# Gated mixer trunk, one core: the stage between the last block and the output projection rearranged, low parts of mixed tiles 4 to 7 on POOL

## The reference, cut to what matters

```
mixed = sum over n of sigmoid(h @ w_gate[n] + b_gate[n]) * (o[n] @ w_branch[n])
x = x + gate1 * (mixed @ w_out)
x = x + gate2 * conv_ffn(rms_norm(x) * (1 + scale2) + shift2)
out = rms_norm(x)
```

## Time and profile before

| | us |
|---|---|
| median of 3 runs (lowest, highest) | 2003.59 (2002.2, 2004.47) |
| the profiled execution, its own time | 2004.98 |
| span of its profile | 2003.1 |
| PE busy in the span | 1891.8 (94%) |
| POOL busy | 909.0 (45%) |
| DVE busy | 930.9 (46%) |
| ACT busy | 471.6 (24%) |

### The profile page before, as it was taken

How to read it: one execution, slowest core, us unless ns; L and a number is a source line. 1 busy time by engine, 2 the same in 40 slices (tenths; PEclk the granted TensorE clock), 3 DMA queues, 4 the chain that set the end, 5 groups by cost and what they waited for, 6 DMA issues and landing times.

```text
span 2003.1 us, 33657 instructions
## 1 busy us (share of the span) xinstructions
PE 1891.8 (94%) x14012; PEld 1511.2 (75%) x14012; DVE 930.9 (46%) x1470; ACT 471.6 (24%) x732; POOL 909.0 (45%) x1100
## 2 busy tenths in 40 slices
PE   4998899998999999999997799999999999999995
PEld 2886677767788878887885677788888888888884
DVE  5455669855454544544543824532332322323325
ACT  4313444442221312212212302410110100101003
POOL 1675456521332323323232475365564655646554
PEclk7999899999999999999998899999999999999998
DMA  8472211221312212212115631011111111111112
GB/s 324 136 236 84 74 53 64 96 98 53 98 39 88 78 54 93 67 60 85 44 60 194 229 107 53 21 43 52 45 50 52 42 52 52 42 52 43 52 42 84
DMA packets 70497, 164.98 MB, mean 82 GB/s; under 512 B 6000, under 2 KB 31088, under 8 KB 70384
## 3 DMA queue, kind: packets, MB, share of 16 engines
q1 hardware_dynamic: 62896, 144.45, 22.0%
q10 hardware_dynamic: 7488, 18.88, 2.6%
HBM read 133.95 MB, written 29.36 MB: 82 GB/s over the span
## 4 chain that ended last, share of the span: by engine, by line
PE 46%; POOL 22%; issue 19%; DVE 5%; ACT 3%; DMA 3%; SPq 1%; POOLq 0%; ACTq 0%; DVEq 0%
PE gbank L550 32%; POOL w_hi L467 11%; POOL w_lo L471 11%; PE mbank L867 3%; DMA fa<-in_w_ada 1%; DVE fa L1730 1%; PE gbank L867 1%; PE mbank L624 1%; DMA fa<-mix_scr 1%; PE gbank L645 1%; DVE fa L1669 1%; PE mbank L790 1%; PE mbank L964 1%; POOL fa L530 1%; PE mbank L633 1%
## 5 line engine op out<-in xcount | busy, mean ns | idle before, releaser
L467 POOL TENSOR_TENSOR w_hi<-w_raw,zero 128x256 fp32r<-128x256 f32 (+1 forms) x528 | 402.7, 793 | 1014.0 <-PE gbank L550 820.5
L550 PE MATMUL gbank<-h_hi,w_hi 128*128 128x512 f32 x1696 | 675.7, 398 | 10.0 <-POOL w_lo L471 6.1
L550 PE MATMUL gbank<-h_hi,w_lo 128*128 128x512 f32 x1696 | 675.2, 398 | 0.0
L550 PE MATMUL gbank<-h_lo,w_hi 128*128 128x512 f32 x1696 | 671.9, 396 | 0.0
L471 POOL TENSOR_TENSOR w_lo<-w_raw,w_hi 128x256 fp32r<-128x256 f32 (+1 forms) x528 | 467.2, 915 | 10.3
L550 PEld LDWEIGHTS gbank<-h_hi,w_hi 128*128 128x128 f32 x1696 | 320.8, 189 | 91.9 <-issue 19.0
L550 PEld LDWEIGHTS gbank<-h_hi,w_lo 128*128 128x128 f32 x1696 | 320.7, 189 | 70.2 <-issue 3.1
L550 PEld LDWEIGHTS gbank<-h_lo,w_hi 128*128 128x128 f32 x1696 | 320.9, 189 | 66.8 <-issue 1.4
L1088 PE MATMUL mbank<-ra,w_hi 128*128 128x512 f32 x640 | 197.1, 389 | 0.0
L1088 PEld LDWEIGHTS mbank<-ra,w_hi 128*128 128x128 f32 x640 | 120.1, 188 | 24.9
L2115 DVE SCALAR_TENSOR_TENSOR fa<-mbank,mod,fa 128x1024 f32<-128x1024 f32 x40 | 51.4, 1284 | 169.2 <-PE mbank L1088 169.2
(11 more groups left out here) (324 smaller groups left out, 2078.9 us busy)
## 6 DMA issues: line engine op xcount, KB each, us to landing
w_raw<-in_w_tail SPq DMA_DIRECT2D x74, 512.0 KB, 3.6
fa<-in_w_ada SPq DMA_DIRECT2D x48, 512.0 KB, 5.2
w_raw<-in_w_in SPq DMA_DIRECT2D x26, 512.0 KB, 3.6
p_scr<-fa ACTq DMA_DIRECT2D x20, 512.0 KB, 2.6
w_raw<-in_w_mix SPq DMA_DIRECT2D x16, 640.0 KB, 3.8
fa<-in_xT SPq DMA_DIRECT2D x16, 512.0 KB, 8.5
fa<-p_scr SPq DMA_DIRECT2D x8, 1024.0 KB, 5.7
w_raw<-in_w_gate SPq DMA_DIRECT2D x16, 512.0 KB, 4.9
```

What stands on the lines that cost most here:

```text
L467: last = pool.tensor_tensor(hi[:, c], raw[:, c], zero[:, 0:1].to_broadcast([P, w]), ALU.add)
L550: mm = pe.matmul(gb[bank], w, r, start=(q == 0), stop=(q == 3 * ks - 1))
```

## The change

It rewrites the stage after the last block, and leaves the arithmetic as it is.

- **Places in `fa`.** The tiles are laid out anew, so that what is dead before the last block ends lies in tiles 0 to 11. The `mix` tile is tile 7: the last block's mixed columns stay there, as tile m = 7.
- **o.** The first 896 columns (blocks 0 to 6) are loaded during block 7 (`o_in`), and their high and low parts are made by ACT and DVE inside block 7; the last 128 columns come straight from the block's tiles. The stores of block 7 are gone.
- **Loads.** The first four gate tiles (now tiles 8 to 11) and the mixed tiles are loaded during block 7 as well, in SP's queue between the `w_branch` units.
- **Branch weights.** Units 60 and 61 are split into `h_hi`/`h_lo` tiles 6 and 7, which are free until mixed tiles 6 and 7 are made, so they wait for no product. Unit 62 then waits for product 4, unit 63 for product 8.
- **First output tile.** Its matmuls go to `mbank`, and those for mixed tile k = 0, 1, 2 stand between products: after products 11, 13 and 15; k = 3 to 7 follow. In the PE's queue `first_out_tile(0)`, which waits for the split of unit 62, stands ahead of product 12.
- **SP's queue.** Unit 61 is fetched after the gate tiles for products 4 to 7, unit 62 after those for 8 to 11 (the last waits for the sum of product 7), unit 63 after those for 12 to 15 (the last waits for the sum of product 11).
- **Low parts of the mixed tiles.** DVE makes those of tiles 0 to 3; POOL makes those of tiles 4 to 7, each in four pieces of 256 columns, in its queue behind the split of unit 63.

```diff
+        O_COLS = (NB - 1) * P
+        o_room = [r_.rearrange("p (t c) -> p t c", t=2) for r_ in (flat[:, 0:2 * O_COLS], flat[:, 2 * S:2 * S + 2 * O_COLS])]
+        GATE_TILE = 8
...
@@ SP
-            for n in range(2):
-                unit("w_branch", n, n, U_BR + n)
-            block_out(NB - 1)
-            sp.wait_ge(sem("gated"), 4 * NB)
-            sp.wait_ge(sem("block_stored"), 48 * NB)
-            sp.wait_ge(sem("sig_stored"), 64 * NB)
...
+            sp.wait_ge(sem("block_stored"), 48 * (NB - 1))
+            sp.wait_ge(sem("pblk_read"), NB)
+            o_in(0)
+            sp.wait_ge(sem("rw_p3"), at("rw_p3", NB - 1))
+            o_in(1)
+            unit("w_branch", 0, 0, U_BR)
...
+            sp.wait_ge(sem("r3"), at("r3", NB - 1))
+            sp.wait_ge(sem("sig_stored"), 64 * (NB - 1))
             for s_ in range(4):
+                if s_ == 2:
+                    sp.wait_ge(sem("gated"), 4 * NB)
+                gate_in(s_ // 2, s_)
+            sp.dma_start(fa[:, 4:7, :], mix_scr[4:7].rearrange("t p c -> p t c")).then_inc(sem("mix_in1"), 16)
+            sp.wait_ge(sem("o_lo"), 2)
+            sp.dma_start(fa[:, 0:4, :], mix_scr[0:4].rearrange("t p c -> p t c")).then_inc(sem("mix_in0"), 16)
+            unit("w_branch", 1, 1, U_BR + 1)
+            unit("w_branch", 2, 0, U_BR + 2)
             for un in range(1, 4):
-                if un >= 2:
-                    unit("w_branch", un, un % 2, U_BR + un)
                 for s_ in range(4):
                     sp.wait_ge(sem("mixed"), 4 * un + s_ - 3)
+                    if un == 3 and s_ == 2:
+                        sp.wait_ge(sem("sig_stored"), 64 * NB)
+                    gate_in(2 * un + s_ // 2, s_)
+                if un == 1:
+                    unit("w_branch", 3, 1, U_BR + 3)
+                else:
+                    unit("w_tail", un - 2, un % 2, U_OUT + un - 2)
@@ POOL
             for un in range(4):
-                used = (sem("gb2_full"), U_BR - 1 + un) if un < 2 else (sem("br_full"), 4 * un - 4)
-                split(U_BR + un, un % 2, 16 * ((U_BR + un) // 2 + 1), used=used)
+                to = None if un < 2 else (h_hi[:, 4 + un, :], h_lo[:, 4 + un, :])
+                split(U_BR + un, un % 2, 16 * ((U_BR + un) // 2 + 1), used=(sem("gb2_full"), min(U_BR - 1 + un, U_BR)), to=to)
+            def mixed_lo(k):
+                pool.wait_ge(sem("mixed_lo"), k)
+                pool.wait_ge(sem("mixed_hi"), k + 1)
+                for c in [slice(n * 256, (n + 1) * 256) for n in range(4)]:
+                    last = pool.tensor_tensor(h_lo[:, k, c], fa[:, k, c], h_hi[:, k, c].bitcast(F32), ALU.subtract)
+                last.then_inc(sem("mixed_lo"), 1)
             for m in OUT_ORDER:
...
-                    used = (sem("br_full"), 12 + 4 * m) if m < 2 else (sem("half_done"), 2 * m - 2)
+                    used = (sem("br_full"), 4 + 4 * m) if m < 2 else (sem("half_done"), 2 * m - 2)
...
                 split(u, u % 2, 16 * (u // 2 + 1), used=used, to=to)
+                if m == 1:
+                    for k in range(KT // 2, KT):
+                        mixed_lo(k)
@@ PE
+            def branch_product(t):
...
+                if t % 4 == 0:
+                    pe.wait_ge(sem("w_split"), U_BR + 1 + un)
+                if t < 2:
+                    pe.wait_ge(sem("o_lo"), 3 + br)
+                else:
+                    pe.wait_ge(sem("gated"), 4 * NB + t - 1)
...
+            def first_out_tile(k):
+                if k == 0:
+                    pe.wait_ge(sem("w_split"), OUT_POS[0] + 1)
...
+                pe.wait_ge(sem("mixed_lo"), k + 1)
...
+            for t in range(2 * KT):
+                branch_product(t)
+                if t >= 11 and t % 2:
+                    first_out_tile(t // 2 - 5)
+            for k in range(3, KT):
+                first_out_tile(k)
@@ ACT, block 7 only: ahead of gate_raw(4), behind gate_raw(6), ahead of gate_raw(7)
+                    act.wait_ge(sem("gb1_full"), 4 * NB)
+                    for n in range(2):
+                        act.wait_ge(sem(f"o_in{n}"), 16)
+                        act.activation(ra[:, 4 * n:4 * n + 2, 0:O_COLS], o_room[n], ACT.Copy).then_inc(sem("o_hi"), 1)
...
+                    last_o_hi(0, "gd_o", gd["o"])
...
+                    last_o_hi(1, "rw_o", rw["o"])
@@ DVE, block 7 only: o_lo(0) behind new_values(0), o_lo(1) behind next_state(0), last columns behind gd_o and rw_o
+                def o_lo(n, nth, cols, o_):
+                    dve.wait_ge(sem("o_hi"), nth)
+                    dve.tensor_tensor(ra[:, 4 * n + 2:4 * n + 4, cols], o_, ra[:, 4 * n:4 * n + 2, cols].bitcast(F32),
+                                      ALU.subtract).then_inc(sem("o_lo"), 1)
...
-                if m:
+                if 1 <= m <= KT // 2:
                     mixed_lo(m - 1)
-            mixed_lo(KT - 1)
```

More of the change, by code:

```diff
@@ L234, in room, with rooms @@
             return names[name]
[L236 to L247, removed]
+        rw, gd = {}, {}
+        def rooms(table, prefix, *entries):
+            for n_, c_ in entries:
+                table[n_] = room(prefix + n_, c_)
@@ L1011, in out_unit @@
-            def out_unit(m, slot, first):
+            def branch_product(t):
+                m, br = divmod(t, 2)
+                un, c = m // 2, m % 2 * 512 + br * 256
+                hi, lo = (w_hi[:, un, :], w_lo[:, un, :]) if un < 2 else (h_hi[:, 4 + un, :], h_lo[:, 4 + un, :])
+                if t % 4 == 0:
[4 more added lines that the diff above has]
+                    pe.wait_ge(sem("gated"), 4 * NB + t - 1)
+                for hf in range(2):
+                    for k in range(2):
+                        for which in range(3):
+                            w = (lo if which == 2 else hi)[:, c + k * P:c + (k + 1) * P]
+                            r = ra[:, 4 * br + (2 if which == 1 else 0) + k, hf * HALF:(hf + 1) * HALF]
+                            mm = pe.matmul(gb[2 * br + hf], w, r, start=(k == 0 and which == 0), stop=(k == 1 and which == 2))
+                mm.then_inc(sem("br_full"), 1)
@@ new lines, in first_out_tile @@
+            def first_out_tile(k):
+                if k == 0:
+                    pe.wait_ge(sem("w_split"), OUT_POS[0] + 1)
+                    pe.wait_ge(sem("rw_rno"), at("rw_rno", NB - 1))
+                    pe.wait_ge(sem("rw_o"), at("rw_o", NB - 1))
+                pe.wait_ge(sem("mixed_lo"), k + 1)
+                for hf in range(2):
+                    for which in range(3):
+                        w = (w_lo if which == 2 else w_hi)[:, 0, k * P:(k + 1) * P]
+                        r = (h_lo if which == 1 else h_hi)[:, k, hf * HALF:(hf + 1) * HALF]
+                        mm = pe.matmul(mb[hf], w, r, start=(k == 0 and which == 0), stop=(k == KT - 1 and which == 2))
+                    if k == KT - 1:
+                        mm.then_inc(sem("half_done"), 1)
@@ L1451, in _ @@
                 gate_raw(6)
+                if not ahead:
+                    last_o_hi(0, "gd_o", gd["o"])
                 act.wait_ge(sem("rw_m2"), at("rw_m2", i))
@@ L1977, in _ @@
                     prep_bonus(i + 1)
+                else:
+                    o_lo(0, 1, slice(0, O_COLS), o_room[0])
                 dve.wait_ge(sem("rw_dec"), at("rw_dec", i))
@@ L1981, in _ @@
                     prep_decayed(i + 1)
+                else:
+                    o_lo(1, 2, slice(0, O_COLS), o_room[1])
                 new_values(1)
@@ L1995, in _ @@
                 dve.tensor_tensor(gd["o"], gd["o"], gd["z"], ALU.mult).then_inc(done("gd_o", i), 1)
+                if not ahead:
+                    o_lo(0, 3, slice(O_COLS, S), t2(gd["o"]))
                 dve.wait_ge(sem("rw_rno"), at("rw_rno", i))
```

105 lines of the change are left out of this document (41 added, 64 removed).

## The result

| | before | after |
|---|---|---|
| median (lowest, highest), us | 2004.03 (2002.2, 2006.35) | 1982.91 (1980.62, 1983.97) |
| ratio, 95% interval | | 0.9892 [0.9875, 0.991] |
| profiled execution: span, us | 2003.1 | 1982.2 |

The forecast was 1980.9 with a range of 1976 to 1988. The kernel is 21 us faster, and the stage accounts for all of it: from the start of `gate_raw(7)` to DVE's reading of the second half of output tile 0 it was 90.27 us and is 69.27. In what follows this is "the stage". Where the two readings are one row of x2, the second starts 0.66 us after the row.

A forecast was written before the change was run, and what follows sets the result against it. The PE bounds the kernel, but in the stage after the last block it loses time to three waits (26.3 us) and a lower clock. 2004.98 - 22.7 = 1982.3, with the median 1.4 below: 1980.9 us, range 1976 to 1988.

The forecast's parts named there:

- Part 1: Block 7: loading and converting o there costs nothing, with 0.5 and 0.4 us of cover; product 0 starts at 1079.2.
- Part 2: The products: PE paces two tiles, then DVE at 6.04 to 6.47 us each; the 7.2 us wait is gone.
- Part 3: Unit 62, before product 12: its split takes 9.0 us, PE waits 6.3 us and loses the clock for 12 matmuls.
- Part 4: Unit 63 and POOL's four low parts end at 1144.5, the stage at 1146.0: a gain of 22.7 us.
- The price of a shared operation: POOL's work beside DVE: each DVE operation with both operands in SBUF costs POOL 0.96 us.
- Part 5: Output projection after the stage: unit 64 is ready 0.3 us before the PE needs it, so nothing is given back.
- 1 (hindered all the way): POOL's split and low parts cost what contended rows say: gain 10.6 us, time 1993.0; chance 0.14.
- 2 (not hindered): POOL's splits and low parts are not slowed by DVE: gain 27.5 us, time 1976.1; chance 0.09.
- 3: Block 7 or the output projection pays, through late low parts of o or unit 64: some 4 us, 1985; chance 0.13.
- 4: Short PE waits before most products hold the clock at 1.2 GHz from product 4 on: 36 us, 2017; chance 0.04.

The follow-up runs named there:

- e7_o_behind: Changed kernel, but ACT and DVE make the high and low parts of o's first 896 columns behind block 7, units 59 and 60 fetched first: 1993.33 us.
- e10_changed: The changed kernel without any edit, timed again on the same chip as `e11_both_again`: 1983.35 us, ratio to before 0.9898.
- e1_low_dve: Changed kernel, but DVE makes all eight low parts of the mixed tiles and POOL none: 1981.05 us, ratio to before 0.9877.
- e6_no_interleave: Changed kernel, but the matmuls of output tile 0 stand behind all 16 products: 1980.13 us in one run.
- e2_psum_sum: Changed kernel, but DVE's sum reads an idle PSUM bank in place of the mixed tile, so the result is wrong: 1976.87 us in one run.
- e9_shared: Changed kernel, units 62 and 63 fetched four gate tiles earlier, POOL making low parts of tiles 4 and 5, DVE those of 6 and 7: 1976.42 us.
- e5_slots: Changed kernel, but branch weights are split into the two old slots and the first output tile stands behind all products: 1983.34 us in one run.
- e4_both: Changed kernel, but units 62 and 63 fetched four gate tiles earlier and all low parts on DVE: 1975.71 us, ratio to before 0.9847.
- e11_both_again: The edits of `e4_both` on the changed kernel, timed again on one chip with `e10_changed`: 1976.31 us, ratio to before 0.9858.

## Why the prediction was right

The mechanism came as described, step by step. The time is 2.0 us above the point, inside the range. After's trace already stands 0.52 us behind before's when the stage begins (1078.97 against 1078.45); what follows takes that off.

- **Part 1** held. Block 7 paid nothing for o. Product 0 starts at 1079.3 for 1079.2. The covers left (0.56 and 0.27 us) are as thin as forecast (0.5 and 0.4). `e7_o_behind` prices them: 9.6 us with the same work behind the block.
- **Part 2** held in kind, and **its size is the largest miss**. There is no wait before product 8 or 12 for a branch weight. But DVE's tiles 2, 3 and 4 take 6.85, 7.06 and 6.46 us where 6.04, 6.47 and 6.47 were taken, and tile 5's four operations 6.0 for 5.0. The sum of product 11 ends at 1120.6 for 1117.9: 2.7 us late, in `e10_changed` 1.5. I had let POOL pay for the shared operations and DVE only by the one contended cycle of the earlier trace rows. The earlier trace rows had more to say: its two low parts took 3.38 us beside the split, 1.69 each, where alone one takes 1.22.
- **Part 3**: the wait is 4.4 us for 6.3, in `e10_changed` 5.6. Unit 62's split took 8.1 us for 9.0: three operations lie wholly in it, and the fourth, which begins 0.7 us before its end, was itself held back. In `e10_changed` four lie in it and it takes 9.2. Since DVE was later, so was product 11, which the PE ends at 1115.6. The clock was lost for seven or eight matmuls and not twelve (in `e10_changed` some fourteen). All of this lies on the PE's own chain, which did not decide: in after the PE waits for POOL three times more, the last wait until 1146.5.
- **Part 4**, the chain that decided: in after start late by 2.7, landing 4.3 us for 5.4, split 7.25 for 6.2 (two sums in it, one counted), low parts 13.4 for 14.5 (two sums in them, three counted). 2.7 - 1.1 + 1.05 - 1.1 = 1.5; the last low part ends at 1145.95 for 1144.5. The last six matmuls take 1.7 us for 1.4. So the stage is 21.0 us shorter, not 22.7. In `e10_changed` the terms come out nearer: start late by 1.4, landing 4.9, split 6.2, low parts 14.4 with three sums; it ends at 1145.4, and the stage is 21.6 shorter. The misses of the four terms partly cancel, and in after they do so by luck.
- **The price of a shared operation** was 0.96 us of POOL's time. After's rows have (8.1 - 5.15) / 3 = 1.0, those of `e1_low_dve` (9.2 - 5.15) / 4 = 1.0, and `e6_no_interleave` against after (13.42 - 11.38) / 2 = 1.0. It was right, and not the whole bill: DVE pays too, between nothing and 0.6 us. Of the 14 sums and low parts that lie wholly beside POOL in after's stage, four take 1.23 us, as alone, and the longest 1.80; the mean is 0.3 over 1.22.
- **Part 5** held: the PE meets no wait behind output tile 1 that before had not. Unit 64 landed at 1152.1, and with a split of 5.2 it is ready 1.5 us before the PE needs it (1148.0 + 10.9); 0.3 were forecast.
- **Rivals.** 1 (hindered all the way) did not come: two sums fell into POOL's low parts (three in `e10_changed`), and a low part took at most 3.8 us and not 5.7. 2 (not hindered) is what `e2_psum_sum` made: 1976.9 for 1976.1, with a wait for unit 62 that rival 2 did not have. 3 did not come. Of 4 nothing is seen: behind the waits of about 1 us before products 8 and 10 the clock stays up; what the stage's 0.98 lacks is the seven or eight matmuls. It would have decided from 113 matmuls on.

The rule of "SBUF — State Buffer", section "Who interferes with whom" in the Trainium skill gave 1981.9 where the measured size gave 1980.9, and the time is 1982.9. That is no test between the two, since other terms missed by as much. The kind of the rule is borne out by `e2_psum_sum`: with one operand in PSUM, DVE cost POOL nothing. Its form, exclusion for the whole instruction with the later one blocked, fits what both sides pay: DVE 0 to 0.6 us, no more than the 0.6 to 0.7 that one piece of POOL's takes, POOL 1.0, and now the one, now the other for the same encounter. That it is so is inferred from these times, not shown. "GPSIMD Engine Reference", section "Engine selection" in the Trainium skill, advised VectorE for such work. By `e1_low_dve` that alone brings 2.0 to 2.6 us of stage; the wait for unit 62 is still 5.6 us there, and with the early fetches 1.7. `e9_shared` shows that it matters for tiles 6 and 7 only.

What stays open: one run stands for each of `e2_psum_sum`, `e5_slots` to `e9_shared`, so differences under 4 us in their times say little. In the traces of the changed forms other than `e7_o_behind` the stage starts anywhere between 1077.3 and 1080.6 us, with the same work ahead of it; why is not known. Their verdicts rest on the stage, and the stage of one kernel came out 0.6 us apart in two traces, its wait for unit 62 1.2 us apart. The edit of `e2_psum_sum` with early fetches was not tried.

## What to carry to other kernels

When waits are removed, list what each engine's queue does next and price the first item that is late: here it was a fetch which SP could only issue behind a gate tile, and issuing it four gate tiles earlier brought 6.9 of the 9.3 us of stage that were left. When two engines share work, charge the shared operations to both. Profile the same kernel twice before a difference of 1 us in one wait is put down to an edit: here the wait for unit 62 went from 4.4 to 5.6 us with no edit at all. And judge an interleaving only together with what it waits for: taking it out shortened the stage by 2.3 to 2.9 us in one form of the kernel and lengthened it by 2.1 in the other.

## What was not expected of the hardware

- **A collision costs both sides.** A DVE operation of 128x1024 with two operands in SBUF takes 1.22 us alone and 1.23 to 1.81 beside POOL's work, 1.5 in the mean, and one that lies wholly beside it adds 1.0 to POOL: together some 1.3 us beyond the operation's own time. With one operand in PSUM neither pays (1.21 and 5.1).
- **What a wait costs behind it is not in proportion to its length.** Waits of 1.7 and 2.2 us left the granted clock at 1.00 (2.4 GHz). Waits of 2.5 us (`e6_no_interleave`), 2.8 and 5.35 (`e7_o_behind`) and 4.4 (after) each cost seven or eight matmuls at the lower level (1.2 GHz), some 0.2 us each; 4.8 cost ten (`e2_psum_sum`), and before's 5.9 twelve, its 7.2 fourteen and its 13.2 ten. A wait of 5.6 cost fourteen in `e10_changed` and `e1_low_dve` and nine in `e7_o_behind`. So in these traces the time that a cut wait gives back jumps somewhere between 2.5 and 2.2 us. The window behind the 2.5 us wait:

```profile
1133.76:1137.70 3.94, 3.79 (x9) 2.56 (x10) 0.00 (x0) 0.00 (x0) 3.83 (x6) 0.57 0.58 147
```

  Why the same 5.6 us cost nine matmuls once and fourteen twice is open.
- **The same waits later cost different times.** From the end of the stage to the end of the span, the changed kernel took 834.0 us and `e4_both` 835.8, with the same waits there (6.3, 6.2, 4.2 and 2.1 us). Part of the difference stands in the matmuls behind the 3.5 us waits; in after, then in `e4_both` (line, instruction, count, busy us, mean ns, idle before):

```profile
L1111 PE MATMUL gbank<-h_hi,ra 128*128 128x512 f32 x64 | 23.9, 445 | 6.4 <-DVE h_lo L2139 6.3
L1111 PE MATMUL gbank<-h_lo,ra 128*128 128x512 f32 x32 | 13.8, 430 | 0.0
```

```profile
L1108 PE MATMUL gbank<-h_hi,ra 128*128 128x512 f32 x64 | 24.9, 461 | 6.4 <-DVE h_lo L2137 6.3
L1108 PE MATMUL gbank<-h_lo,ra 128*128 128x512 f32 x32 | 14.2, 445 | 0.0
```

1.4 us of the 1.8 are there. `e11_both_again` has the same 835.8 and the same two rows; `e9_shared`, whose stage is as short, has 834.0. That the lower clock is what lengthens them is argued from the mean, not shown. It goes with the medians, where a stage 8.7 to 9.3 us shorter made the runs only 7 us shorter.
- **The same fetch lands at different times.** 512 KB landed 4.3 us after the issue in after (unit 63), 4.45 (unit 62), and 7.2 in `e2_psum_sum` (unit 62), with the same transfers ahead of it in SP's queue. The cause is not shown.
